# A two-layer hybrid backbone block on one core: the transform table asked for ahead of the filter rows, value folds and inverse split by parity, and longer unread fillings

## The reference

```
layer 0: u = modulate(rmsnorm(h)); y = concat(GLA(u, ctx), hyena(u)) @ w_out; h += gate * y
         hyena: p0, p1, v = split(dwconv3(u @ w));  y = p0 * (bidir_fftconv(v * p1, filters) )
         filters = sine-MLP(position) @ w3 * window            (1024 x 2 x 512)
layer 1: u = modulate(rmsnorm(h)); y = (bg * dwconv3(cg * xin)) @ w_out; h += gate * y
both:    v = modulate(rmsnorm(h)); top-1 group, top-2 of its 8 experts; h += gate * sum(expert(v))
out = rmsnorm(h)
```

## Time and profile before

| | us |
|---|---|
| median of 3 runs | 2666.64 (2656.6 to 2668.95) |
| the profiled execution, its own time | 2666.26 |
| its span (first to last instruction) | 2664.3 |
| TensorE matmul busy | 2459.2 (92%) |
| VectorE / ScalarE / GpSimd busy | 1018.8 / 332.4 / 152.8 |
| DMA | 572.04 MB, mean 215 GB/s |
| mean granted TensorE clock | 0.956 of 2.4 GHz |

### The profile page before, as it was taken

One profiled execution on the slowest core, in us unless ns is written; L12 is line 12 of the kernel. 1 busy time (PEld: TensorE's weight loads), 2 busy tenths in 40 slices (PEclk: granted clock), 3 DMA queues, 4 the chain that ended last, 5 costly groups with the idle time before them and its releaser, 6 DMA issues. The chain is left out here.

```text
span 2664.3 us, 32938 instructions
## 1 busy us (share of the span) xinstructions
PE 2459.2 (92%) x14399; PEld 1109.7 (42%) x14400; DVE 1018.8 (38%) x2030; ACT 332.4 (12%) x648; POOL 152.8 (6%) x171
## 2 busy tenths in 40 slices
PE   5999998969999899999999799999999999999991
PEld 3455444535555533333333544444555333333330
DVE  2787477726846422222121411011464222222214
ACT  2211233320011100000000410000111000000001
POOL 2000000001000000000000000000000000000000
PEclk9999999986999899999999899999998999999995
DMA  9575001010120799999997701010007999999975
GB/s 338 182 259 196 16 24 30 34 71 32 63 87 32 284 349 397 388 390 395 381 369 304 236 24 47 24 55 32 24 32 294 373 390 384 385 393 383 395 280 214
DMA packets 121869, 572.04 MB, mean 215 GB/s; under 512 B 11744, under 2 KB 48808, under 8 KB 94713
## 3 DMA queue, kind: packets, MB, share of 16 engines
q1 hardware_dynamic: 104328, 526.47, 51.6%
q0 software_dynamic: 17312, 43.16, 4.1%
q10 hardware_dynamic: 80, 0.26, 0.0%
HBM read 548.61 MB, written 38.01 MB: 220 GB/s over the span
## 5 line engine op out<-in xcount | busy, mean ns | idle before, releaser
L1608 PE MATMUL ps<-arena 128*32 128x512 f32 x6144 | 693.2, 604 | 28.5 <-DMA arena<-in_ex_w_dram 27.9
L1608 PEld LDWEIGHTS ps<-arena 128*32 128x32 f32 x6144 | 200.2, 112 | 453.5 <-issue 452.2
L1632 PE MATMUL ps<-arena 128*32 128x512 f32 x3072 | 343.4, 599 | 8.9 <-DMA arena<-in_ex_w_dram 8.8
L1710 PE MATMUL ps<-arena 128*128 128x512 f32 x768 | 330.4, 593 | 4.5 <-ACT arena L1003 4.5
L2315 DVE TENSOR_SCALAR arena<-ps,gain_x,mod 128x128 f32<-128x128 f32 x384 | 126.8, 403 | 373.4 <-PE ps L1593 373.4
L1473 PE MATMUL ps<-arena 128*128 128x512 f32 x512 | 226.6, 597 | 2.9 <-DVE arena L2116 1.6
L1710 PEld LDWEIGHTS ps<-arena 128*128 128x128 f32 x768 | 146.0, 190 | 186.3 <-issue 186.3
L1632 PEld LDWEIGHTS ps<-arena 128*32 128x32 f32 x3072 | 108.4, 111 | 234.7 <-issue 234.7
L2347 DVE SCALAR_TENSOR_TENSOR arena<-ps,arena,gates 128x512 f32<-128x512 f32 x96 | 72.1, 751 | 263.9 <-PE ps L1632 263.9
L1284 PE MATMUL ps<-arena 128*128 128x512 f32 x384 | 167.3, 594 | 0.7 <-issue 0.7
L2323 DVE TENSOR_TENSOR arena<-arena,ps 128x512 f32<-128x512 f32 x48 | 52.6, 1095 | 276.0 <-PE ps L1608 276.0
(11 more groups left out here) (287 smaller groups left out, 2078.8 us busy)
## 6 DMA issues: line engine op xcount, KB each, us to landing
arena<-in_ex_w_dram SPq DMA_DIRECT2D x192, 2048.0 KB, 11.9
arena<-in_mod_w_dram SPq DMA_DIRECT2D x24, 2048.0 KB, 8.7
arena<-expert_rows SPq DMA_DIRECT2D x16, 1024.0 KB, 8.6
arena<-in_od_w_in_dram SPq DMA_DIRECT2D x24, 512.0 KB, 6.4
arena<-in_x_dram SPq DMA_DIRECT2D x2, 4096.0 KB, 15.0
normed_rows<-arena POOLq DMA_DIRECT2D x16, 512.0 KB, 2.9
arena<-in_ev_w_in_dram SPq DMA_DIRECT2D x3, 2048.0 KB, 13.0
arena<-in_ev_w_in_dram SPq DMA_DIRECT2D x12, 512.0 KB, 4.2
```

The lines of the kernel that those rows point to most:

```text
L1608: ins = nc.tensor.matmul(bank(2 + m)[c:c + n], x[:, j, c:c + n], w_slot(e % 2, m, KC, FE)[:, j], start=j == 0, stop=j == KC - 1)
L1632: ins = nc.tensor.matmul(bank(5 + half)[c:c + n], HT[:, j * P + c:j * P + c + n], w_slot(e % 2, 2, FC, D)[:, j, half * 512:(half + 1) * 51 ...
L1710: ins = nc.tensor.matmul(bank(2 * k + half), slab(L1_IN + c, 3, KC, P)[:, k, j], u_part(half, j), start=j == 0, stop=j == KC - 1)
```

## The change

- SyncE asks for the `DFT` table directly behind the wait for the last hyena projection, ahead of the two filter loads and their waits.
- The residues fill banks 0 to 7 in order (before: 4 to 7, then 0 to 3); the wait for `omix_ready` moves from i = 2 to i = 0.
- `USUM[1]` is laid out so that even rows lie where `VTM` of parity 0 was and odd rows where parity 1 was. The folds i = 0, 1 of g = 1 then wait for 12 residues instead of 16, and filter rows 0 and 1 wait for folds 10 and 12 instead of 14 and 16.
- The product folds are made in two halves of four; the inverse goes parity by parity, and each parity waits only for its half. The final VectorE steps follow in that order.
- Fillings: modulation 4 to 7 (three times); in `mix_and_route` 4 to 6 ahead of `places(TT - 2)` and 1 to 2 ahead of the last `logits` (each layer); 2 to 11 ahead of `turn(0)` and 12 to 18 ahead of the last `pass_down` (each layer); 10 new ones ahead of the wait for `ov_left` in `shortconv`.

```diff
-        USUM = [at(0, 8, HW), at(34816, 8, HW)]
+        USUM = [at(0, 8, HW), at(34816, 2, 4, HW)]
+        def usum(g, q):
+            return USUM[1][:, q % 2, q // 2] if g else USUM[0][:, q]
...
             sp.wait_ge(hy_mm, 6 * HC)
+            sp.dma_start(at(12288, 8192), a["dft"]).then_inc(tables_in, 16)
             sp.wait_ge(flt_in, 64)
             sp.wait_ge(vx_ready, HC)
             sp.dma_start(HH2[0:HID], filter_hidden).then_inc(flt_in, 16)
             sp.dma_start(W3H[0:HID], a["hy_w3"][0]).then_inc(flt_in, 16)
-            sp.dma_start(at(12288, 8192), a["dft"]).then_inc(tables_in, 16)
...  modulation
-                        spare(4, 7)
+                        spare(7, 7)
...  residue (and ScalarE, VectorE: bank((2 * i + 4) % 8) becomes bank(2 * i))
-                elif i == 2:
+                elif i == 0:
                     pe.wait_ge(omix_ready, 2 * HEADS)
...  filter rows on TensorE
-                        pe.wait_ge(butterfly, 14 + 2 * t)
+                        pe.wait_ge(butterfly, 10 + 2 * t)
...  inverse
                 for g in range(2):
-                    pe.wait_ge(butterfly, folds_before(2 * g + 2))
-                    for c in range(HC):
-                        for par in range(2):
+                    for par in range(2):
+                        pe.wait_ge(butterfly, folds_before(2 * g + 2) - 4 + 4 * par)
+                        for c in range(HC):
                             if g == 0:
                                 pe.wait_ge(butterfly, folds_before(2 + c // 2) + 4)
...  mix_and_route
-                spare(4, 2)
+                spare(6, 2)
                 places(TT - 2)
-                spare(1, 2)
+                spare(2, 2)
                 logits(TT - 1)
...  experts
                 table_of_gates(l)
-                spare(2, 2)
+                spare(11, 2)
                 turn(0)
...
-                spare(12, 0)
+                spare(18, 0)
                 pass_down(NP - 1)
...  shortconv
+                spare(10, 0)
                 pe.wait_ge(ov_left, 5)
...  value folds on VectorE
-                    dve.wait_ge(dft_mm, 16 if g else 2 * (i + 1))
+                    dve.wait_ge(dft_mm, (12 if i < 2 else 16) if g else 2 * (i + 1))
...  product folds on VectorE
-                    for p, q, sign in pairs:
-                        V.tensor_tensor(p, p, q, ...)
-                    for n, (p, q, sign) in enumerate(pairs):
-                        dve.wait_ge(butterfly, folds_before(kt) + 4 + n + 1)
-                        V.scalar_tensor_tensor(out=q, in0=q, ...)
+                    for m in (0, 2):
+                        for p, q, sign in pairs[m:m + 2]:
+                            V.tensor_tensor(p, p, q, ...)
+                        for n, (p, q, sign) in enumerate(pairs[m:m + 2]):
+                            dve.wait_ge(butterfly, folds_before(kt) + 4 + 2 * m + n + 1)
+                            V.scalar_tensor_tensor(out=q, in0=q, ...)
```

More of the change, by code:

```diff
@@ L973, in _ @@
                         act.wait_ge(butterfly, 2 * (i + 1))
-                    nc.scalar.activation(USECOND[:, i], bank((2 * i + 4) % 8 + 1), ACT.Copy).then_inc(uk_ready, 1)
+                    nc.scalar.activation(USECOND[:, i], bank(2 * i + 1), ACT.Copy).then_inc(uk_ready, 1)
             for t in range(2 * KT):
@@ L1382, in residue @@
                     pe.wait_ge(butterfly, 2 * (i + 1))
-                elif i == 2:
+                elif i == 0:
                     pe.wait_ge(omix_ready, 2 * HEADS)
                 for tc in (2 * s, 2 * s + 1):
-                    ins = nc.tensor.matmul(bank((2 * i + 4) % 8 + s), DFT[:, 2 * g, fn, par, tc * P:(tc + 1) * P], VTM[:, par, tc],
+                    ins = nc.tensor.matmul(bank(2 * i + s), DFT[:, 2 * g, fn, par, tc * P:(tc + 1) * P], VTM[:, par, tc],
                                            start=tc == 2 * s, stop=tc == 2 * s + 1)
@@ L2034, in _ @@
             for g in range(2):
-                u = USUM[g]
                 for i, (plus, minus, turned) in enumerate(((0, 4, 0), (2, 6, 1), (1, 7, 0), (3, 5, 0))):
-                    dve.wait_ge(dft_mm, 16 if g else 2 * (i + 1))
+                    dve.wait_ge(dft_mm, (12 if i < 2 else 16) if g else 2 * (i + 1))
                     dve.wait_ge(uk_ready, 4 * g + i + 1)
-                    first, second = bank((2 * i + 4) % 8), USECOND[:, i]
-                    V.tensor_tensor(u[:, plus], first, second, ALU.add).then_inc(butterfly, 1)
+                    first, second = bank(2 * i), USECOND[:, i]
+                    V.tensor_tensor(usum(g, plus), first, second, ALU.add).then_inc(butterfly, 1)
                     if turned:
                         first, second = second, first
-                    V.tensor_tensor(u[:, minus], first, second, ALU.subtract).then_inc(butterfly, 1)
+                    V.tensor_tensor(usum(g, minus), first, second, ALU.subtract).then_inc(butterfly, 1)
             dve.wait_ge(tables_in, 32)
@@ L2061, in _ @@
                     for fn in range(2):
-                        a, b = USUM[g][:, 4 * half + 2 * fn], USUM[g][:, 4 * half + 2 * fn + 1]
+                        a, b = usum(g, 4 * half + 2 * fn), usum(g, 4 * half + 2 * fn + 1)
                         V.tensor_tensor(a, a, b, ALU.add).then_inc(butterfly, 1)
@@ L2074, in _ @@
                 dve.wait_ge(butterfly, folds_before(kt) + 4)
-                u, y = USUM[kt // 2][:, 4 * (kt % 2):4 * (kt % 2) + 4], YF[:, kt]
+                u, y = [usum(kt // 2, 4 * (kt % 2) + q) for q in range(4)], YF[:, kt]
                 if kt:
@@ L2079, in _ @@
                     t0, t1 = (PTMP[row // 2][:, q] for q in range(2))
[L2080 to L2083, removed]
+                    step(V.tensor_tensor(y[:, row + 1], u[0], w[:, second], ALU.mult))
+                    step(V.tensor_tensor(y[:, row], u[2], w[:, 2 - second], ALU.mult))
+                    n = step(V.tensor_tensor(t0, u[1], w[:, second + 1], ALU.mult))
+                    step(V.tensor_tensor(t1, u[3], w[:, 3 - second], ALU.mult))
                     settle(n)
@@ L2098, in _ @@
                     pairs = ((y[:, 0], z[:, 0], 1), (y[:, 2], z[:, 2], -1), (y[:, 1], z[:, 3], 1), (y[:, 3], z[:, 1], 1))
-                    for p, q, sign in pairs:
-                        V.tensor_tensor(p, p, q, ALU.add if sign > 0 else ALU.subtract).then_inc(butterfly, 1)
-                    for n, (p, q, sign) in enumerate(pairs):
-                        dve.wait_ge(butterfly, folds_before(kt) + 4 + n + 1)
[L2103 to L2108, removed]
+                    for m in (0, 2):
+                        for p, q, sign in pairs[m:m + 2]:
+                            V.tensor_tensor(p, p, q, ALU.add if sign > 0 else ALU.subtract).then_inc(butterfly, 1)
+                        for n, (p, q, sign) in enumerate(pairs[m:m + 2]):
+                            dve.wait_ge(butterfly, folds_before(kt) + 4 + 2 * m + n + 1)
+                            V.scalar_tensor_tensor(out=q, in0=q, scalar=-2.0 * sign, in1=p, op0=ALU.mult, op1=ALU.add)\
+                                .then_inc(butterfly, 1)
+            for par in range(2):
+                for c in range(HC):
+                    n, m = 2 * c + par, HC * par + c
+                    dve.wait_ge(idft_mm, m + 1)
                     sl = slice(par, SEQ - 1 + par, 2)
-                    tmp = CTMP[:, n % 2]
-                    if c:
-                        dve.wait_ge(hmix_ready, n - 1)
+                    tmp = CTMP[:, m % 2]
+                    if m >= 2:
+                        dve.wait_ge(hmix_ready, m - 1)
                     link(V.scalar_tensor_tensor(out=tmp, in0=VX[:, c, sl],
```

## The result

The kernel after takes 2628.58 us (median of 4 runs, 2625.69 to 2630.25) beside 2663.23 for the kernel before (4 runs): ratio 0.987 [0.9842, 0.9897]. On two more chips it was 0.9863 [0.9819, 0.9908] and 0.9882 [0.9857, 0.9906]. The medians differ by 34.7 us here and by 39.1 and 32.0 on the other two chips; 27.6 was forecast. The profiled execution took 2629.31 us (span 2627.5), 36.95 less than that of before; the steps are followed in these two. Lines of the kernel after are 4 higher than before in most of TensorE's code.

The account below looks back on a forecast made before the run. TensorE, busy 92% of the span, was taken as the bound: its busy time, gaps and low clock. Gains of 38.6 us less losses of 11.0 took 2666.3 to 2638.7 us, predicted 2639, range 2628 to 2653.

Parts of the forecast that it names:

- table: start of residues, and their length: Long convolution: the table lands earlier, so residues start 14.15 us sooner; 0.2 more from the clock, 14.3 in all.
- folds by parity, filter rows: Filter rows: the 3.86 us gap goes and the full clock holds about 14 us; 14.6 us gained, gap included.
- inverse: Inverse of the long convolution: gap shrinks from 5.56 to about 2 us, clock stays up; 2.4 + 2.8 = 5.2 gained.
- last passes, both layers: Last `pass_down`: six more fillings inside waits for the last weights hold the clock; 1.7 + 2.8 = 4.5 us gained.
- modulation: Modulation: nine more fillings, 3.5 us on the path plus 0.6 for the fourth slab; 4.1 us lost.
- `turn(0)`, layers 0 and 1: Ahead of the first pass: nine more fillings delay `turn(0)`; 1.9 us lost in layer 0, 5.0 in layer 1.
- fillings in routing and ahead of `shortconv`: Ahead of `places`, last `logits` and in `shortconv`: fillings lie in idle gaps; nothing gained or lost.
- expert stages ahead of the last pass: Expert passes before the last: no gain or loss in the sum; predicted 0.
- the bound of 17.3: Filter rows: if the clock stays, VectorE is the bound, spectra start 29.9 us after the residues; 17.3 us gained.
- the one with the clock to the end: Filter rows: full clock throughout, 17.3 us gained, spectra 1.5 more; 2634.5 us, chance 0.18.
- the one with the early fall: Filter rows: clock falls within the first few us, 5.7 us gained instead of 14.6; 2647.6 us, chance 0.27.
- The slower rival: Expert stages: a later start adds waits for weights, 3.6 us each; with 14 more, 2689 us; chance 0.03.

Follow-up runs that it names:

- e1: The kernel before with only SyncE's request for the transform table moved early; 2645.07 us, ratio 0.995.
- e2: The kernel after with all five filling counts back to those of before; 2618.62 us, ratio 0.9861.
- e3: The kernel after with the folds again waiting for all 16 residues and filter rows for all eight folds; 2649.68 us, ratio 0.9965.
- e6: The kernel after with fillings cut in modulation and ahead of `turn(0)`, new ones behind the filter rows' gate parts; 2619.18 us, ratio 0.9833.
- e4b: The kernel after with e3's waits put back and six fillings in the gap ahead of the filter rows, run again for its profile; 2630.45 us (one run).
- e6b: The kernel of e6 run again beside the kernel after on one chip; 2614.47 us, ratio 0.9826.
- e5: The kernel after with four fillings in modulation and two ahead of `turn(0)`, as before, other fillings kept; 2621.61 us, ratio 0.9847.

## Why the prediction was right, and where its sizes were off

Between the two profiles, in the terms of the sum:

| term | predicted | measured |
|---|---|---|
| table: start of residues, and their length | +14.3 | +14.2, + 1.4 |
| folds by parity, filter rows | +14.6 | +18.8 |
| inverse | +5.2 | +3.4 |
| last passes, both layers | +4.5 | +4.5 |
| modulation | -4.1 | -3.4 |
| `turn(0)`, layers 0 and 1 | -1.9, -5.0 | -1.4, -5.5 |
| fillings in routing and ahead of `shortconv` | 0 | +0.2, -0.2 |
| expert stages ahead of the last pass | 0 | +5.0 |
| sum | 27.6 | 37.0 |

- The table: as predicted, what is late next is ScalarE's last copy, 0.69 us behind its transposes. The clock at the start of the residues came back somewhat earlier than taken (0.90 against 0.82 in the first 16 us): 1.4 us instead of 0.2. This is not the table's work: with the table alone (e1) the residues took 30.75 us. In every kernel with the new bank order and the moved wait for `omix_ready`, e2 without the longer fillings too, they took 29.1 to 29.4. Which of the edits brings it no run shows.
- The folds: the mechanism held, its size did not, and this is 4.2 of the 9.4 us by which the sum missed. The step taken was that the clock holds until TensorE meets pauses, 14 us in. It held 21.5 us, and fell 2 us after the first pause. Two numbers behind that were wrong. TensorE's slack against VectorE was taken to show as pauses from about 13 us on; the first came 19 us in, 0.65 us long. (By the code a filter row waits only for the row two before it, so TensorE can run ahead that far.) And the bound of 17.3 (spectra 29.9 us after the residues) was passed: VectorE did begin 2.7 us after the residues (585.23), but its first row took 2.0 us instead of 3.1, and the spectra wait for the last windowing (L2060), not for the 0.6 us gate copy behind it: 29.9 less 1.7 is the measured 28.3.
- Of the rivals the one with the clock to the end was the nearest in time (2634.5), though the clock did fall, at 604 us; the one with the early fall is refuted: 64-row matmuls that came in at 2.4 GHz kept it, in e1 and e3 those that came in at 1.2 GHz kept that, with no pause in either.
- The Trainium skill (TensorE: Matmul & The Clock Gate, Part 1) has it that sustained activity releases the throttle and idleness brings it back. Going down the traces agree in part: with TensorE's pauses filled in e6 the clock stayed to the end of the stage, but in the kernel after one pause of 0.65 us stood ahead of the fall at 604. Going up they don't: 43 us of these matmuls in e1 were busy and stayed at 1.2 GHz.
- The inverse: the gap is as predicted, 1.98 and 0.91 us. The clock's term was too large: it fell all the same, and of 2.8 us 1.0 came. Nine profiles have this inverse: in e3, e4b, e6 and e6b the last group took 14.1 us, in e2, e5 and the three of the kernel after 15.8, behind the same gap of 1.98: what decides it is open.
- Fillings: all four terms within 0.8 us. Those in modulation and ahead of `turn(0)` of layer 1 lie bare on the path, as priced. The means over more profiles are 3.3, 1.0 and 4.3 us; of layer 1's the size is loose, since the same code took 9.99 to 13.34 us with the short fillings and 13.88 to 17.18 with the long ones. The fillings in routing and ahead of `shortconv` cost nothing, as taken: the latter halved the gate parts behind them (7.09 to 3.78 us), and the stage took 539.1 and 539.3 us.
- The expert stages: the 5.0 us are not the change's. e1, whose code there is that of before, was 5.4 and 4.9 us shorter than before in the same stages. How often the clock fell there goes with it: eight times before, five after, four in e1, each time at a wait for weights of 1.95 to 2.92 us. The slower rival, which needed 14 more such waits, found two more (17 against 15 at the line shown). So without this share the sum would have been 32.0: 4.4 above the forecast, not 9.4.

## What to carry to other kernels

A short gap ahead of a long run of matmuls that don't raise TensorE's clock themselves is worth several times its length: in e3 5 us of gap cost 15 us of clock. Look at the record lengths behind each gap before pricing it, and cover it (an earlier wait, or fillings into a spare bank). A filling is free only where the timeline shows idle time behind it: lengthen it there, and shorten it where nothing is waited for.

## What was not expected of the hardware

- The same eight 64-row records took 3.82 us or 7.18, for as long as 20 and 43 us without a change of level; which of the two was set by what ran just ahead of them. Twelve records of 128x256 in front (2.83 us, e4b) were enough to keep the upper level.
- VectorE's and GpSimd's windowing seem to hold each other up, and who pays goes with a few hundredths of a us in their starts. VectorE's and then GpSimd's timeline in the profile after:

```profile
586.65 0.69 DVE L2060 TENSOR_TENSOR arena<-arena 128x512 f32<-128x512 f32 x1
...
588.67 1.76 DVE L2060 TENSOR_TENSOR arena<-arena 128x512 f32<-128x512 f32 x1
```

```profile
586.69 1.77 POOL L719 TENSOR_TENSOR arena<-arena 128x512 f32<-128x512 f32 x1 [69.19 <-DVE arena L2056]
588.62 1.26 POOL L719 TENSOR_TENSOR arena<-arena 128x512 f32<-128x512 f32 x1 [0.15 <-DVE arena L2056]
```

The first time VectorE starts 0.04 us ahead: 0.69 us for it, 1.77 for GpSimd. Then GpSimd starts 0.05 us ahead, and takes 1.26 us, VectorE 1.76; so it stays for the seven other rows, in eleven of the profiles, that of the kernel before among them. At 1.1 us each this is 7.5 us of the stage in which VectorE is now the bound. Since only the first row differs, no run here separates the order of the starts from its being the first, and none ran one engine's windowing without the other's.
- The stage of `shortconv`, with layer 1's routing, took 534 to 544 us over twelve profiles, whose code there differs only by ten fillings ahead of it and three in the routing (mean 540 with and without the ten). The clock falls at its pauses in some executions and not in others: its mean over the stage was 0.99 in the 534.1 us of the second profile of the kernel after, 0.97 in the 543.8 us of e6. Single profiles can't tell changes of a few us behind such places.
